# Neighbourhood attention: the product of weights and reciprocal sums on GpSimd instead of VectorE

## The chip, the cores and the metric

The kernel runs on one core of one Trainium2 chip. The metric is the device time of one execution in microseconds (us). Before the change three runs took 2624.79, 2625.38 and 2626.43 us; the median is 2625.38 us.

## The reference, cut to what matters

The program computes two blocks of a network on 512 tokens of 1024 features in float32: four mixers (retention with neighbourhood attention, a state-space mixer, latent attention, an mLSTM) and four feed-forward layers. The change touches the first mixer alone, and in it the neighbourhood attention on the grid of 8 rows by 64 columns:

```
sc = einsum('brqhd,brwchd->bhrqwc', qb, kb) + bias      # a query sees 8 rows x 16 columns
sc = where(valid, sc, -inf)
pr = softmax(sc)                                        # exp(sc - max) / sum
return einsum('bhrqwc,brwchd->brqhd', pr, vb)
```

Beside it the mixer's other half, retention, ends in a normalisation over each head (`mu`, `var`, `rsqrt`), a gain and a gate; then `concatenate([ret_out, na_out]) @ w_out` follows.

## The kernel before, in words

The program is written engine by engine, with the order of each engine's instructions and all semaphores by hand. Most of its time is TensorE's: products of weight blocks with activations, each split in a high and a low part.

The neighbourhood attention is 16 items (`NA_ITEMS`): four pairs of heads by four blocks of 16 query columns. An item has two heads, e = 0 and 1, and for each 128 queries by 256 keys. The engines go over the items in step n:

- TensorE (`pe_softmax`, step n): waits for the maxima of item n-1 (`item_max`), multiplies queries and keys of item n into bank 0 and bank 1 (L1295, the scores); multiplies the turned weights of item n-3 with the values (L1326); waits for each head's normalised weights of item n-2 (`item_normed`) and transposes them (L1315); then runs the hook.
- VectorE (`dve_softmax`, step n): for each head adds the bias table to the scores and takes the maximum in one instruction (L1376); negates the two maxima (L1380, `item_max`); then, for item n-1, takes the reciprocal of the two sums (L1387) and multiplies the weights by it, one instruction of 128x256 for each head (L1389, `item_normed`); then runs the hook.
- ScalarE (`act_softmax`, step n): copies the transposed weights of item n-2 from their bank (L1351), takes the exponential of item n with its sum (L1360, two heads), then runs the hook.

Three buffers hold the weights (`na_soft`), two hold each item's columns of maxima and sums (`stat`).

The hooks carry the normalisation of the retention half, in six steps for each of four feature tiles j (`gn_steps`): in step 3j+2 TensorE multiplies by a centring matrix (L1646) and ScalarE copies the result (L1665); GpSimd squares it (L1720); in step 3j+5 TensorE takes the variance (L1649); in step 3j+6 ScalarE takes the reciprocal root in two instructions (L394, L395); in step 3j+7 VectorE multiplies by it and by gain and gate (L1657, L1658). Four copies of finished outputs by ScalarE (L1706), and in two steps the split of an output tile for the next product (ScalarE L592, then VectorE L597), are in the hooks too. From step 15 on TensorE fills gaps with the next product (`ab_out`, L374 to L376).

GpSimd (`pool_na_tables`) builds the bias tables for all eight heads (L1727, 24 instructions), which ends before the items need them, and then has only the four squares left in this stage. Items 0 and 1 are started inside the last two steps of the retention loop, where L1612 is VectorE's work.

Of the kernel before, what the change touches and what calls it, by code (L numbers as in the profile page):

```python
# [165 lines left out]
def build(nc, A, stop=None):  # L166

    with ExitStack() as ctx:
        sems = {}

        def sem(name):
            if name not in sems:
                sems[name] = ctx.enter_context(nc.semaphore(name))
            return sems[name]
# [707 lines left out]
            return 32 * f + m + 1  # L882

        POOL_SUMS, COPIES, DVE_SUMS = 1 + 4 * PAIRS + MLP_TILES, 5 + 2 * PAIRS, 7 + 2 * PAIRS
        TOKEN_SUMS = ("t3", "t1", "t2", "t4")
        SUM_AT = {"s1": 0, "s2": 1, "s3": 2, "s4": 3}

# [10 lines left out]
            return COPIES * f + 5 + 2 * n + 2  # L898

        def w_summed(f, n):  # L900
            return DVE_SUMS * f + 7 + 2 * n + 1

        def c_summed(f, n):
            return DVE_SUMS * f + 7 + 2 * n + 2

        def token_low(f, t):
            return DVE_SUMS * f + 3 + TOKEN_SUMS.index(t) + 1

        TOKEN_AT = {"t4": 0, "t3": 1, "t1": 2, "t2": 3}
        HALF_N = SEQ // 2  # L910
# [48 lines left out]
        def pool_pairs(pool, f):  # L959
            pool.wait_ge(sem("sum_copied"), COPIES * f + 1)  # L960
            pool.wait_ge(sem("norm_added"), 6 + 2 * f)
            b = over_a[:, :].rearrange("p (k s) -> p k s", k=4)
            pool.tensor_tensor(mT[:, token("t1")].rearrange("p (k s) -> p k s", k=4), b[:, :, HALF_N:SEQ], b[:, :, 0:HALF_N],
                               ALU.subtract).then_inc(sem("sum_pool"), 1)
            pool.wait_ge(sem("sum_pool"), POOL_SUMS * f + 1)
            pool.wait_ge(sem("sum_dve"), DVE_SUMS * f + 1)
            for n in range(PAIRS):
                wait_block(pool, f, n, 0)
                wait_block(pool, f, n, 1)
                if n:  # L970
                    pool.wait_ge(sem("w_lo"), split(f, "s1", n - 1))
                pool.tensor_tensor(sum_raw("s1"), block_raw(f, n, "a21"), block_raw(f, n, "a22"), ALU.add)\
                    .then_inc(sem("sum_pool"), 1)
                if n:
                    pool.wait_ge(sem("w_lo"), split(f, "s2", n - 1))
                pool.wait_ge(sem("sum_pool"), pool_summed(f, "s1", n))
                pool.tensor_tensor(sum_raw("s2"), sum_raw("s1"), block_raw(f, n, "a11"), ALU.subtract)\
                    .then_inc(sem("sum_pool"), 1)
                if n:
                    pool.wait_ge(sem("w_lo"), split(f, "s3", n - 1))  # L980
                pool.tensor_tensor(sum_raw("s3"), block_raw(f, n, "a11"), block_raw(f, n, "a21"), ALU.subtract)\
                    .then_inc(sem("sum_pool"), 1)
                if n:
                    pool.wait_ge(sem("w_lo"), split(f, "s4", n - 1))
                pool.wait_ge(sem("sum_pool"), pool_summed(f, "s2", n))
                pool.tensor_tensor(sum_raw("s4"), block_raw(f, n, "a12"), sum_raw("s2"), ALU.subtract)\
                    .then_inc(sem("sum_pool"), 1)

            pool.wait_ge(sem("norm_rstd"), 6 + 2 * f)
            for m in range(MLP_TILES):  # L990
                pool.wait_ge(sem("mlp_hidden"), relu_done(f, m))
                pool.tensor_tensor(tile(m), tile(m), rstd[:, :], ALU.mult).then_inc(sem("sum_pool"), 1)  # L992

        def act_mlp_up(act, f):
# [7 lines left out]
            def token_high(t):  # L1002
                if t == "t1":
                    act.wait_ge(sem("sum_pool"), POOL_SUMS * f + 1)
                else:
                    act.wait_ge(sem("sum_dve"), DVE_SUMS * f + {"t3": 1, "t2": 2, "t4": 3}[t])
                act.activation(tok_hi[:, token(t)], mT[:, token(t)], ACT.Copy).then_inc(sem("sum_copied"), 1)

            def high(q, n):
# [107 lines left out]
        def dve_mlp_up(dve, f):  # L1117
# [3 lines left out]
            def tokens(t):  # L1121

                half = slice(0, HALF_N) if t == "t4" else slice(HALF_N, SEQ)
                if t == "t3":
                    dve.wait_ge(sem("sum_copied"), COPIES * f + 1)
                if t == "t2":
                    dve.wait_ge(sem("sum_pool"), POOL_SUMS * f + 1)
                if t == "t4":
                    dve.wait_ge(sem("sum_dve"), DVE_SUMS * f + 2)
                    dve.wait_ge(sem("norm_sum"), norm + 1)  # L1130
                for j in range(4):
                    less = over_a[:, j * SEQ + HALF_N:(j + 1) * SEQ] if t == "t3" else mT[:, token("t1" if t == "t2" else "t2", j)]
                    ins = dve.scalar_tensor_tensor(out=mT[:, token(t, j)], in0=xt(4 + j)[:, half], scalar=col(g, g0 + 4 + j),
                                                   in1=less, op0=ALU.mult, op1=ALU.subtract)
                ins.then_inc(sem("sum_dve"), 1)

            def token_lows(t):
                dve.wait_ge(sem("sum_copied"), COPIES * f + 1 + TOKEN_SUMS.index(t) + 1)
                if t == "t1":
                    dve.wait_ge(sem("sum_dve"), DVE_SUMS * f + 2)  # L1140
                if t == "t2":
                    dve.wait_ge(sem("sum_dve"), DVE_SUMS * f + 3)
                dve.tensor_tensor(tok_lo[:, token(t)], mT[:, token(t)], tok_hi[:, token(t)], ALU.subtract)\
                    .then_inc(sem("sum_dve"), 1)

# [215 lines left out]
                                       scale=items[n]["scale"][e], accum_out=stat(1, n, e)).then_inc(sem("item_exp"), 1)  # L1361
                hook(act, n)

        def dve_softmax(dve, n0, items, soft, ready, hook, part=None):
            N = len(items)
            lo, hi = part or (0, N + 1)
            for n in range(lo, hi):
                if n < N:
                    it = items[n]
                    w = it["w"]  # L1370
                    ready(dve, n)
                    if n >= 3:
                        dve.wait_ge(sem("item_transposed"), n0 + n - 2)
                    for e in range(2):
                        dve.wait_ge(sem("item_scored"), 2 * (n0 + n) + e + 1)
                        dve_order(dve, dve.tensor_tensor_reduce(out=soft(n, e)[:, 0:w], in0=bank[e][:, 0:w], in1=it["bias"][e],  # L1376
                                                                scale=1.0, scalar=NEG, op0=ALU.add, op1=ALU.max,
                                                                accum_out=stat(2, n, e)))
                    if it["minus"] is None:
                        dve.tensor_scalar(stat(0, n, 0, 2), stat(2, n, 0, 2), -1.0, None, ALU.mult).then_inc(sem("item_max"), 1)  # L1380
                    else:
                        dve.tensor_tensor(stat(0, n, 0, 2), stat(2, n, 0, 2), it["minus"], ALU.mult).then_inc(sem("item_max"), 1)
                if n >= 1:
                    m = n - 1
                    w = items[m]["w"]
                    dve.wait_ge(sem("item_exp"), 2 * (n0 + m) + 2)
                    dve_order(dve, dve.reciprocal(stat(3, m, 0, 2), stat(1, m, 0, 2)))  # L1387
                    for e in range(2):
                        dve.tensor_scalar(soft(m, e)[:, 0:w], soft(m, e)[:, 0:w], stat(3, m, e), None, ALU.mult)\  # L1389
                            .then_inc(sem("item_normed"), 1)  # L1390
                hook(dve, n)

        def stat(kind, n, e, count=1):
            c = 4 + kind * 4 + n % 2 * 2 + e
            return stats[:, c:c + count]
# [314 lines left out]
        def pool_na_tables(pool):  # L1710
# [4 lines left out]
            def squares(j):  # L1715
                pool.wait_ge(sem("gn_centered"), j + 1)
                if j:
                    pool.wait_ge(sem("gn_var"), j)
                y = tile(RV + j)
                pool.tensor_tensor(sq[:, 0:SEQ], y, y, ALU.mult).then_inc(sem("gn_sq"), 1)  # L1720

            for h in range(8):
                if h in (4, 6):
                    pool.wait_ge(sem("ret_scored"), 8 * (h // 2))
                for v, shift in enumerate((16, 8, 0)):
# [2 lines left out]
                                       wide(arena[:, a:a + 1], [15, SPAN], [1, ROWS]),  # L1728
                                       wide(ab["namask"][:, v * 256:v * 256 + 1], [8, SPAN], [1, ROWS]), ALU.add)\
                        .then_inc(sem("na_table"), 1)  # L1730
            for j in range(4):
                squares(j)

        def pe_ab_up(pe):
            def between(pe, m):
# [24 lines left out]
        def dve_na(dve, part):  # L1760
            def ready(dve, n):
                dve.wait_ge(sem("na_table"), 6 * (n // 4) + 6)
                if n == 1:
                    dve.wait_ge(sem("ret_valued"), 15)

            def hook(dve, n):
                gn_dve(dve, n)
                if n in (11, 14):
                    dve_low_part(dve, "ab_out", At(n // 3 - 3))
            dve_softmax(dve, 0, NA_ITEMS, na_soft, ready, hook, part)  # L1770

        def pe_ab(pe):
            pe_retention(pe)
# [1672 lines left out]
```

## Time and profile before

| | before |
|---|---|
| median of three runs | 2625.38 us |
| the profiled execution's own time | 2624.66 us |
| its span | 2622.7 us |
| TensorE busy | 2583.3 us (98%) |
| VectorE busy | 1682.1 us (64%) |
| ScalarE busy | 1287.1 us (49%) |
| GpSimd busy | 503.7 us (19%) |
| first scores of the attention | 203.06 us from the span's start |
| scores of its last item | 241.51 us |

The span is the profiled part of an execution. Busy shares are means over all stages. TensorE's granted clock is at its full level through the span (mean 0.998). In the timelines below an instruction's start is the time from the span's start, and its end is the start plus the duration; where two instructions are merged (x2), the duration is that of both. TensorE's ends are modelled, and its rows may overlap by some tenths of a microsecond.

### The profile page before, as it was taken

To read this page: it belongs to the slowest core of one execution; us is meant where nothing else is said; L and a number is where in the kernel's file an instruction comes from. 1 tells how busy PE (TensorE), PEld (TensorE's weight loads), DVE (VectorE), ACT (ScalarE), POOL (GpSimd) and SP (SyncE) were. 2 spreads that over 40 slices of the span, in tenths; PEclk is the share of its full clock that TensorE was granted. 3 is DMA by queue.
4 is the path that set the end of the run, shared out by engine and by line. 5 is a ranking of instruction groups with operands and counts; after the bars stand their busy time and mean duration, and the time that the engine had idled before them with its cause. 6 is when DMAs were issued, how large, how long until landed. Compare 5 with 4: busy or idle time off the path is not lost. (4 is left out here: it accounts for less than half of the span.)

```text
span 2622.7 us, 35151 instructions
## 1 busy us (share of the span) xinstructions
PE 2583.3 (98%) x12530; PEld 2047.4 (78%) x12530; DVE 1682.1 (64%) x2288; ACT 1287.1 (49%) x2138; POOL 503.7 (19%) x366
## 2 busy tenths in 40 slices
PE   9999999999999999999999999999999999999999
PEld 7855788888786557788888776789988777889887
DVE  4476677643988785677653787578733536678633
ACT  3326544333547894444333587457533425557432
POOL 0021100000114781100000130035810002045800
PEclk9999999999999999999999999999999999999999
DMA  5320222222244442222222220133232321233222
GB/s 212 105 79 17 95 97 97 98 97 98 82 131 129 121 129 80 81 96 96 96 97 98 92 73 1 65 102 108 83 111 97 103 86 49 97 105 113 81 96 96
DMA packets 72991, 248.39 MB, mean 95 GB/s; under 512 B 8076, under 2 KB 8204, under 8 KB 72496
## 3 DMA queue, kind: packets, MB, share of 16 engines
q1 hardware_dynamic: 71792, 238.53, 27.4%
q0 software_dynamic: 944, 8.40, 0.8%
q8 instruction: 67, 1.10, 0.2%
q14 instruction: 44, 0.36, 0.0%
q10 hardware_dynamic: 144, 0.00, 0.0%
HBM read 242.56 MB, written 2.24 MB: 93 GB/s over the span
## 5 line engine op out<-in xcount | busy, mean ns | idle before, releaser
L356 DVE TENSOR_TENSOR wlo<-wraw,whi 128x1024 fp32r<-128x1024 f32 x357 | 458.2, 1285 | 429.7 <-ACT whi L333 428.8
L374 PE MATMUL bank<-hnhi,whi 128*128 128x512 f32 (+1 forms) x1664 | 654.1, 393 | 2.0 <-DVE arena L1954 1.2
L375 PE MATMUL bank<-hnlo,whi 128*128 128x512 f32 (+1 forms) x1664 | 638.4, 384 | 0.0
L333 ACT ACTIVATE whi<-wraw 128x1024 fp32r<-128x1024 f32 x361 | 379.9, 1055 | 480.6 <-DMA wraw<-in_w 480.5
L376 PE MATMUL bank<-hnhi,wlo 128*128 128x512 f32 x1568 | 611.0, 390 | 0.0
L374 PE MATMUL bank<-ahi,whi 128*128 128x512 f32 x1184 | 463.1, 391 | 1.0 <-DVE alo L597 0.5
L375 PE MATMUL bank<-alo,whi 128*128 128x512 f32 x1184 | 460.9, 389 | 0.0
L376 PE MATMUL bank<-ahi,wlo 128*128 128x512 f32 x1184 | 460.8, 389 | 0.0
L374 PEld LDWEIGHTS bank<-hnhi,whi 128*128 128x128 f32 x1664 | 312.8, 188 | 93.7 <-issue 32.8
L375 PEld LDWEIGHTS bank<-hnlo,whi 128*128 128x128 f32 x1664 | 313.0, 188 | 64.0 <-issue 4.8
L376 PEld LDWEIGHTS bank<-hnhi,wlo 128*128 128x128 f32 x1568 | 294.3, 188 | 62.5
L374 PEld LDWEIGHTS bank<-ahi,whi 128*128 128x128 f32 x1184 | 222.3, 188 | 51.2 <-DVE alo L597 3.8
L376 PEld LDWEIGHTS bank<-ahi,wlo 128*128 128x128 f32 x1184 | 222.2, 188 | 46.5
L375 PEld LDWEIGHTS bank<-alo,whi 128*128 128x128 f32 x1184 | 222.3, 188 | 45.9 <-issue 0.5
L777 POOL TENSOR_TENSOR xT<-xT,mT 128x512 f32<-128x512 f32 x20 | 33.9, 1726 | 873.2 <-DVE mT L769 873.2
L818 ACT ACTIVATE mT<-mT,cols 128x512 f32<-128x512 f32 x88 | 71.8, 816 | 223.3 <-DVE mT L516 223.3
L592 ACT ACTIVATE ahi<-arena 128x512 fp32r (+1 forms) x140 | 87.9, 630 | 136.1 <-PE bank L376 135.0
L597 DVE TENSOR_TENSOR alo<-arena,ahi 128x512 fp32r<-128x512 f32 x140 | 110.4, 788 | 66.7 <-ACT ahi L592 66.5
L841 DVE SCALAR_TENSOR_TENSOR mT<-mT,cols 128x511 f32<-128x511 f32 x88 | 66.1, 751 | 97.3 <-ACT mT L818 97.3
L992 POOL TENSOR_TENSOR arena<-arena,rstd 128x512 f32<-128x512 f32 x64 | 110.7, 1768 | 0.0
L516 DVE TENSOR_TENSOR arena<-bank,rstd 128x512 f32<-128x512 f32 (+3 forms) x48 | 36.5, 763 | 110.3 <-PE bank L376 98.5
L1149 DVE TENSOR_TENSOR quarter_lo<-over_a,whi 128x512 fp32r<-128x512 f32 x96 | 83.5, 873 | 23.6 <-ACT whi L1021 22.9
(350 smaller groups left out, 3894.0 us busy)
## 6 DMA issues: line engine op xcount, KB each, us to landing
wraw<-in_w SPq DMA_DIRECT2D x410, 512.0 KB, 3.3
arena<-cs_scratch SPq DMA_DIRECT2D x20, 512.0 KB, 5.9
over_a<-cs_scratch SPq DMA_DIRECT2D x12, 512.0 KB, 6.1
arena<-in_rpb POOLq DMA_DIRECT2D x1, 2880.0 KB, 14.6
out_dram<-xT SPq DMA_DIRECT2D x8, 256.0 KB, 2.0
arena<-in_t_step POOLq DMA_DIRECT2D x2, 897.0 KB, 5.4
mT<-arena SPq DMA_DIRECT2D x28, 64.0 KB, 2.0
arena<-in_t_ab POOLq DMA_DIRECT2D x1, 1472.0 KB, 7.2
```

Of the source, the lines that this page charges most:

```text
L333: act.activation(whi[:, slot * BLOCK:(slot + 1) * BLOCK], wraw[:, slot * BLOCK:(slot + 1) * BLOCK], ACT.Copy).then_inc(sem("w_hi"), 1)
L356: dve.tensor_tensor(wlo[:, slot * BLOCK:(slot + 1) * BLOCK], wraw[:, slot * BLOCK:(slot + 1) * BLOCK], whi[:, slot * BLOCK:(slot + 1) * BL ...
L374: pe.matmul(out, wh, ah, start=start, stop=False)
L375: pe.matmul(out, wh, al, start=False, stop=False)
L376: return pe.matmul(out, wl, ah, start=False, stop=stop)
L516: dve.tensor_tensor(out, src, by, ALU.mult).then_inc(sem(done), 1)
L592: act.activation(ahi[:, c:c + SEQ], src(k), ACT.Copy).then_inc(sem("a_hi"), 1)
L597: dve.tensor_tensor(alo[:, c:c + SEQ], MIXERS[name][0](k), ahi[:, c:c + SEQ], ALU.subtract).then_inc(sem("a_lo"), 1)
L818: act.activation(cbuf(m), ubuf(m), ACT.Identity, bias=col("fb", m + 44 * f), scale=col("fw", m + (132 * f + 44))).then_inc(sem("ffn_center ...
L841: dve.scalar_tensor_tensor(out=c[:, 1:SEQ], in0=u[:, 0:SEQ - 1], scalar=col("fw", m + 132 * f), in1=c[:, 1:SEQ], op0=ALU.mult, op1=ALU.add ...
L992: pool.tensor_tensor(tile(m), tile(m), rstd[:, :], ALU.mult).then_inc(sem("sum_pool"), 1)
L1149: dve.tensor_tensor(quarter_low(q, n), src, quarter_hi(f, q, n), ALU.subtract).then_inc(sem("w_lo"), 1)
```

## The change: who multiplies, and in which order

VectorE still takes the reciprocal of the two sums (L1387), but signals it to GpSimd through the semaphore `sum_dve` and no longer waits for its own result. The two multiplications of each item go to GpSimd, which waits for that signal and then signals `item_normed` twice. GpSimd's four squares, which stood after the tables, are put behind the multiplications of items 1, 4, 7 and 10. The semaphore `sum_dve` is used later in the program too; its counts there are raised by 16 (`DVE_BASE`), in seven places of which one is shown.

```diff
         def token_low(f, t):
-            return DVE_SUMS * f + 3 + TOKEN_SUMS.index(t) + 1
+            return DVE_BASE + DVE_SUMS * f + 3 + TOKEN_SUMS.index(t) + 1
...
-        def dve_softmax(dve, n0, items, soft, ready, hook, part=None):
+        def dve_softmax(dve, n0, items, soft, ready, hook, part=None, by_pool=False):
...
                     dve.wait_ge(sem("item_exp"), 2 * (n0 + m) + 2)
-                    dve_order(dve, dve.reciprocal(stat(3, m, 0, 2), stat(1, m, 0, 2)))
-                    for e in range(2):
+                    if by_pool:
+                        dve.reciprocal(stat(3, m, 0, 2), stat(1, m, 0, 2)).then_inc(sem("sum_dve"), 1)
+                    else:
+                        dve_order(dve, dve.reciprocal(stat(3, m, 0, 2), stat(1, m, 0, 2)))
+                    for e in range(0 if by_pool else 2):
                         dve.tensor_scalar(soft(m, e)[:, 0:w], soft(m, e)[:, 0:w], stat(3, m, e), None, ALU.mult)\
                             .then_inc(sem("item_normed"), 1)
...
-            for j in range(4):
-                squares(j)
+            for m in range(len(NA_ITEMS)):
+                pool.wait_ge(sem("sum_dve"), m + 1)
+                for e in range(2):
+                    pool.tensor_scalar(na_soft(m, e), na_soft(m, e), stat(3, m, e), None, ALU.mult).then_inc(sem("item_normed"), 1)
+                if m % 3 == 1 and m < 12:
+                    squares(m // 3)
...
-            dve_softmax(dve, 0, NA_ITEMS, na_soft, ready, hook, part)
+            dve_softmax(dve, 0, NA_ITEMS, na_soft, ready, hook, part, by_pool=True)
```

The second user of `dve_softmax`, the latent attention later in the program, keeps the multiplications on VectorE.

## Rows read from the trace of the kernel before

**Rows 1.** Who waited for whom, 203 to 252 us: total us, times, longest us.

```profile
PEld bank L1295 <- DVE stats L1380: 7.2, 12, 1.1
DVE mT L1376 <- PE bank L1295: 5.3, 12, 1.7
```

**Rows 2.** Busy time by stretch: length, PE, PEld, DVE, ACT, POOL, clock, DMA.

```profile
221.96:226.06 4.10, 3.60 (x21) 1.79 (x21) 3.69 (x13) 3.57 (x11) 0.00 (x0) 1.00 0.00 0
228.09:230.12 2.03, 1.88 (x17) 1.14 (x17) 1.72 (x9) 2.02 (x6) 0.00 (x0) 1.00 0.00 0
241.51:250.00 8.49, 8.41 (x59) 5.87 (x58) 5.08 (x17) 5.78 (x14) 0.00 (x0) 1.00 0.01 2
```

**Rows 3.** Timeline of TensorE: start us, us, engine, line; steps 10, 14 and 15.

```profile
228.09 0.70 PE L1295 MATMUL bank<-arena 64*128 64x256 f32 x4 [0.15 <-DVE stats L1380]
229.31 0.66 PE L1315 MATMUL bank<-base_t,mT 128*128 128x128 f32 x4
230.12 0.70 PE L1295 MATMUL bank<-arena 64*128 64x256 f32 x4 [0.15 <-DVE stats L1380]
...
241.51 0.70 PE L1295 MATMUL bank<-arena 64*128 64x256 f32 x4
...
242.73 0.66 PE L1315 MATMUL bank<-base_t,mT 128*128 128x128 f32 x4
```

**Rows 4.** Timeline of VectorE: the plain step 10.

```profile
227.94 0.16 DVE L1387 RECIPROCAL stats<-stats 128x2 f32<-128x2 f32 x1
228.13 0.61 DVE L1389 TENSOR_SCALAR mT<-mT,stats 128x256 f32<-128x256 f32 x2
228.96 0.42 DVE L1376 CUSTOM_DVE_ANT_0 mT<-bank,arena 128x256 f32<-128x256 f32 x1 [0.21 <-PE bank L1295]
...
229.89 0.17 DVE L1380 TENSOR_SCALAR stats<-stats 128x2 f32<-128x2 f32 x1
```

**Rows 5.** Timeline of all engines, steps 7 to 9.

```profile
221.81 0.16 DVE L1387 RECIPROCAL stats<-stats 128x2 f32<-128x2 f32 x1
...
221.99 0.64 ACT L395 ACTIVATE rstd<-rstd 128x512 f32<-128x512 f32 x1
222.00 0.61 DVE L1389 TENSOR_SCALAR mT<-mT,stats 128x256 f32<-128x256 f32 x2
...
222.66 0.69 DVE L1657 TENSOR_TENSOR arena<-arena,rstd 128x512 f32<-128x512 f32 x1
...
224.98 0.17 DVE L1380 TENSOR_SCALAR stats<-stats 128x2 f32<-128x2 f32 x1
...
226.06 0.70 PE L1295 MATMUL bank<-arena 64*128 64x256 f32 x4
...
226.19 0.57 ACT L1665 ACTIVATE arena<-bank 128x512 f32<-128x512 f32 x1
...
226.84 1.04 POOL L1720 TENSOR_TENSOR sq<-arena 128x512 f32<-128x512 f32 x1 [7.37 <-ACT arena L1665]
...
227.86 0.17 DVE L1380 TENSOR_SCALAR stats<-stats 128x2 f32<-128x2 f32 x1
```

**Rows 6.** Timeline of VectorE: steps 14 and 15.

```profile
241.29 0.17 DVE L1380 TENSOR_SCALAR stats<-stats 128x2 f32<-128x2 f32 x1
...
242.09 0.68 DVE L597 TENSOR_TENSOR alo<-arena,ahi 128x512 fp32r<-128x512 f32 x1
```

**Rows 7.** Timeline, VectorE beside GpSimd: step 3, and a later stage.

```profile
211.23 1.04 POOL L1720 TENSOR_TENSOR sq<-arena 128x512 f32<-128x512 f32 x1 [11.16 <-ACT arena L1665]
...
211.48 0.81 DVE L1380 TENSOR_SCALAR stats<-stats 128x2 f32<-128x2 f32 x1
...
299.56 0.75 DVE L435 SCALAR_TENSOR_TENSOR hnlo<-xT,cols,hnhi 128x512 fp32r<-128x512 f32 x1
299.79 8.47 POOL L777 TENSOR_TENSOR xT<-xT,mT 128x512 f32<-128x512 f32 x5 [63.77 <-DVE mT L769]
...
300.88 1.13 DVE L435 SCALAR_TENSOR_TENSOR hnlo<-xT,cols,hnhi 128x512 fp32r<-128x512 f32 x1
```

**Rows 8.** GpSimd's instructions by shape: count, busy us, mean ns, idle before.

```profile
L1727 POOL TENSOR_TENSOR arena<-arena 128x256 f32<-128x256 f32 x12 | 8.1, 706 | 18.0 <-PE bank L1547 18.0
...
L2915 POOL TENSOR_TENSOR arena<-arena 128x256 f32<-128x256 f32 x3 | 3.3, 1106 | 7.1 <-DVE arena L3109 7.1
L2912 POOL COPY arena<-arena 128x512 f32<-128x512 f32 x3 | 1.8, 612 | 68.2 <-DVE arena L3109 68.2
```

More of the change, by code:

```diff
@@ L884, in build @@
         POOL_SUMS, COPIES, DVE_SUMS = 1 + 4 * PAIRS + MLP_TILES, 5 + 2 * PAIRS, 7 + 2 * PAIRS
+        DVE_BASE = 16
         TOKEN_SUMS = ("t3", "t1", "t2", "t4")
@@ L900, in w_summed @@
         def w_summed(f, n):
-            return DVE_SUMS * f + 7 + 2 * n + 1
+            return DVE_BASE + DVE_SUMS * f + 7 + 2 * n + 1
         def c_summed(f, n):
-            return DVE_SUMS * f + 7 + 2 * n + 2
+            return DVE_BASE + DVE_SUMS * f + 7 + 2 * n + 2
         def token_low(f, t):
-            return DVE_SUMS * f + 3 + TOKEN_SUMS.index(t) + 1
+            return DVE_BASE + DVE_SUMS * f + 3 + TOKEN_SUMS.index(t) + 1
         TOKEN_AT = {"t4": 0, "t3": 1, "t1": 2, "t2": 3}
@@ L965, in pool_pairs @@
             pool.wait_ge(sem("sum_pool"), POOL_SUMS * f + 1)
-            pool.wait_ge(sem("sum_dve"), DVE_SUMS * f + 1)
+            pool.wait_ge(sem("sum_dve"), DVE_BASE + DVE_SUMS * f + 1)
             for n in range(PAIRS):
@@ L1005, in token_high @@
                 else:
-                    act.wait_ge(sem("sum_dve"), DVE_SUMS * f + {"t3": 1, "t2": 2, "t4": 3}[t])
+                    act.wait_ge(sem("sum_dve"), DVE_BASE + DVE_SUMS * f + {"t3": 1, "t2": 2, "t4": 3}[t])
                 act.activation(tok_hi[:, token(t)], mT[:, token(t)], ACT.Copy).then_inc(sem("sum_copied"), 1)
@@ L1128, in tokens @@
                 if t == "t4":
-                    dve.wait_ge(sem("sum_dve"), DVE_SUMS * f + 2)
+                    dve.wait_ge(sem("sum_dve"), DVE_BASE + DVE_SUMS * f + 2)
                     dve.wait_ge(sem("norm_sum"), norm + 1)
@@ L1139, in token_lows @@
                 if t == "t1":
-                    dve.wait_ge(sem("sum_dve"), DVE_SUMS * f + 2)
+                    dve.wait_ge(sem("sum_dve"), DVE_BASE + DVE_SUMS * f + 2)
                 if t == "t2":
-                    dve.wait_ge(sem("sum_dve"), DVE_SUMS * f + 3)
+                    dve.wait_ge(sem("sum_dve"), DVE_BASE + DVE_SUMS * f + 3)
                 dve.tensor_tensor(tok_lo[:, token(t)], mT[:, token(t)], tok_hi[:, token(t)], ALU.subtract)\
```

## The prediction

> **What bounds the kernel now.** The page comes first: TensorE is busy for 2583.3 of 2622.7 us, so the whole program has under 40 us of it idle, and what the change can touch lies between 203.06 and about 250 us. I then read that stretch in four views. The waits [rows 1] show what the steps turn on: TensorE's scores wait for VectorE's negated maxima (7.2 us in 12 places), and VectorE's maxima wait for TensorE's scores (5.3 us in 12 places). Nothing there waits for L1389. The table of stretches [rows 2] gives the two sorts of step: a plain one of 2.03 us, and one with the centring and variance products of 4.10 us; ScalarE has 2.02 us of work in the plain one, so it too is nearly full. The timelines give the loop. In step 10 TensorE starts the scores at 228.09, VectorE starts the maximum at 228.96 after standing idle for 0.21 us, starts the negation at 229.89, and TensorE starts the next scores at 230.12 [rows 3, 4]. VectorE's multiplications run from 228.13 to 228.74, in the time that VectorE would spend waiting for those scores. The reader is to see that the plain period is scores, two maxima, negation, and that the removed work is in none of them.
>
> **What the change removes.** Sixteen pairs of L1389, 0.61 us each [rows 4], 9.8 us of VectorE in all, and a wait on the reciprocal. Its worth on the path, by the kind of step:
> - Plain steps: 0. VectorE waits for the scores with or without it, 0.21 us now and about 0.85 us then.
> - Steps 7, 10 and 13, whose hook has L1657: 0. L1389 ends at 222.00 + 0.61 = 222.61, but L1657 needs ScalarE's L395 too, which ends at 221.99 + 0.64 = 222.63; L1657 starts at 222.66 [rows 5]. The cover of the removed work goes and the other wait stands there at the same moment.
> - Step 14, whose hook has L597: the maximum of item 15 could start some 0.3 us earlier, but no scores come after item 15, and ScalarE is still at other work then: 0. If that cover were not there it would be 0.3 us.
>
> **What it adds.** A pair of GpSimd instructions for each item, behind the reciprocal. The trace has no GpSimd instruction with a tensor and a column as inputs. The nearest rows [rows 8]: a copy of 128x512 takes 0.612 us, so half of it, 0.31, bounds one of 128x256 from below; the two-input form of 128x256 takes 0.71 (table building), and 1.11 in a stage where VectorE works beside it, which bounds it from above. I take 0.50, between the halved copy (which halves its fixed part too) and 0.71. The hand-over to GpSimd is 0.08: L1665 ends at 226.76 and L1720 starts at 226.84 [rows 5].
>
> A plain step then: reciprocal done at 227.94 + 0.16 = 228.10, the first head done at 228.10 + 0.08 + 0.50 = 228.68, the second at 229.18. The transposes start at 229.31 [rows 3], the second head's about 0.3 later, at 229.6. So 0.13 us and more to spare: cost 0. At 0.31 each it is 228.80, at 0.71 it is 229.60 (still about 0), at 1.11 it is 230.40, 0.8 late (below, the slow rival). Step 2 has its transposes earlier, and may lose 0.2 us, but the negation of item 3 is held until 212.29 by the first squares in any case [rows 7]: 0. The moved squares wait for L1665 behind the items before them as before, and the next item's reciprocal comes after they end: 0 by themselves.
>
> **The two engines at once.** Step 3 of the trace shows what else comes with it. L1380, a two-column instruction of 0.17 us, took 0.81: it started at 211.48 and ended at 212.29, when GpSimd's L1720 (211.23 + 1.04 = 212.27) had ended. L435, with two tensors in, takes 0.75 alone and 1.13 beside L777 [rows 7]. So some of VectorE's instructions stand still while GpSimd works. (The Trainium skill, "SBUF — State Buffer", section "Who interferes with whom", says that a VectorE instruction with two SBUF inputs, or in a two-port mode, and a GpSimd instruction that reads SBUF exclude each other, whichever begins first. By that rule L1657, L1658, L597 and L1380 are exposed and L1376, which reads a bank, is not; these two row pairs agree. Without the rule's two-input half the next sum would be 0.)
>
> In steps 7, 10 and 13 the pair on GpSimd runs just where L1657 wants to start. Item 6: reciprocal done 221.97, GpSimd's first 222.05 to 222.55, second to 223.05; L1657 wanted 222.66 and starts about 0.39 late. What that costs [rows 5]: the negation of item 8 moves from 224.98 to 225.37; the scores of item 9 come at 226.06 for TensorE's own reasons, so nothing is lost there. But ScalarE's exponential and L1665 follow, L1720 moves from 226.84 to 227.23 and ends at 228.27, and L1380 of item 9, due at 227.86, stands until then: some 0.36 on the path, since the next scores wait for it. The same once more three steps later (0.36). The third time there are no squares, but L1380 of item 14, at 241.29 + 0.17, is only 0.05 us ahead of the scores at 241.51 [rows 3, 6], so 0.39 - 0.05 = 0.34. Then L597: VectorE now starts it right behind the reciprocal at 241.53, GpSimd is held until 242.22, its second head is done at 243.22, and the transposes at 242.73 want it at about 243.0: 0.2. After that TensorE is busy for 8.41 of 8.49 us [rows 2], so a late start there is not made good.
>
> **Sum.** -0 + 0 + 0.36 + 0.36 + 0.34 + 0.2 = +1.3 us. On the profiled execution, 2624.66 + 1.3 = 2625.9; its time lies 0.7 below the median of the runs, so in medians 2625.38 + 1.3 = 2626.7 us. That is +0.05%, well inside the 0.2% (5.3 us) that I take as what a measurement of this kernel tells from no change.
>
> **Rivals.**
> 1. The engines miss each other (time as before, 2625.4). With 0.31 us for one multiplication the pair ends at 222.05 + 0.62 = 222.67, just when L1657 is ready, and every collision above falls away. (The Trainium skill, "GPSIMD Engine Reference", section 4.1, calls one-input work on GpSimd roughly line-rate, which speaks for this rival.) Against it: the halved copy leaves out the fixed part.
> 2. It is faster after all (2623.2). If VectorE's lateness, not ScalarE's L395, set L1657's start, three hooks would give 0.62 us each and the step with L597 0.3: 3 x 0.62 + 0.3 = 2.2 us. For it: L1389 and L395 end within 0.02 us of each other, so the trace alone doesn't say which is the deeper cause. Against it: ScalarE is full in these steps and would have to be earlier as well.
> 3. Slower (2633): GpSimd's multiplication is the new link. It decides from about 0.7 us for one: then reciprocal to second head, 0.08 + 1.4, exceeds the 1.5 us from 228.10 to 229.6. At 1.11 the second head's transposes start at 230.40 and the next scores some 0.25 later, at 230.65 instead of 230.12, so 0.5 us a step over about nine plain steps, 4.6 us; and L1657 finds the lock taken for 0.5 to 1.6 us three times, another 1.5 to 4.8. Together 6 to 9 us, 2631 to 2634. For it: 1.106 us was measured for this size [rows 8]. Against it: that form has two inputs, and the same form took 0.71 elsewhere.
>
> **How the numbers follow.** Forecast (slower by about 1 us, from 0.4 to 2.5) 0.55; rival 1 0.20; rival 2 0.10; rival 3 0.15. The forecast and the first two rivals lie within 0.2% of before; of rival 3 two thirds lie beyond it, and a gain over 5.3 us would need more idle time than ScalarE leaves. So faster 0.02, same 0.87, slower 0.11. The range for eight in ten leaves out the top of rival 3 and the bottom of rival 2, with 0.6 us for the scatter of the runs: 2623.8 to 2631.0.
>
> **What would show it.** In the profile after: plain steps still 2.03 us with VectorE idle for some 0.8 us before L1376; GpSimd's multiplications near 0.5 us each, ending before the transposes start; L1657 (or its idle time) longer or later by 0.4 us behind GpSimd in steps 7, 10 and 13; L1380 of items 9 and 12 over 0.17 us; the last scores near 242.6 instead of 241.51. Plain steps over 2.2 us, or TensorE's L1315 waiting for GpSimd, would prove rival 3; last scores before 241.0, rival 2. The forecast is wrong if the time is outside 2625.8 to 2628.

## The result, and the profile after

Twenty runs of each kernel: before 2625.36 us (2624.36 to 2627.4), after 2628.93 us (2625.83 to 2631.71), ratio 1.0014 with a 95% interval of 1.0008 to 1.002. The change makes the kernel slower by 3.6 us, inside the 0.2% and inside the range of the prediction, but 2.7 times the +1.3 us that was forecast. Beside the experiments further down, one run of the kernel before took 4299.17 us at a mean granted clock of 0.556; it is left out of every ratio.

The profiled execution after took 2630.92 us, with a span of 2629.0 us, 6.3 us more than before. Only half of that is the change's: in the trace the attention takes, from the start of its first scores to the start of its last values, 46.95 us before (203.07 to 250.02) and 50.10 us after (204.75 to 254.85). This length is what I compare from here on. It is the same within 0.03 us in a second profile of the changed kernel (50.07), where whole runs of one kernel differ by up to 6 us. The rest of the 6.3 us, 1.68 us ahead of the attention and 1.47 behind it, stands where no code changed; the last section says what it is.

Who waited for whom in the stage after, 203 to 256 us (columns as in [rows 1]):

```profile
POOL mT L1738 <- DVE stats L1389: 14.5, 15, 7.6
DVE mT L1377 <- PE bank L1296: 14.2, 13, 2.6
...
PEld bank L1296 <- DVE stats L1381: 5.1, 7, 1.1
PEld bank L1316 <- POOL mT L1738: 4.1, 8, 0.7
```

Against [rows 1], TensorE's scores wait less for the negation (7 times for 12), and a wait is new: the transposes, L1316, wait for GpSimd's multiplication, L1738. Lines have moved: the scores are L1296, the negation L1381, the reciprocal L1389, the hook's L1657 and L1658 are L1661 and L1662.

The stretches that answer to [rows 2], step 8, step 10 and what follows the last scores:

```profile
225.52:229.52 4.00, 3.82 (x22) 1.78 (x21) 2.55 (x8) 3.40 (x12) 2.73 (x3) 1.00 0.00 0
231.55:233.91 2.36, 2.02 (x16) 1.12 (x16) 1.12 (x7) 2.33 (x7) 2.05 (x3) 1.00 0.00 0
245.54:254.03 8.49, 7.94 (x56) 5.46 (x56) 3.59 (x10) 5.78 (x14) 5.83 (x6) 1.00 0.01 2
```

The plain step went from 2.03 to 2.36 us, the long one from 4.10 to 4.00. Step 10 in the timeline, which answers to [rows 3, 4]:

```profile
231.41 0.15 DVE L1389 RECIPROCAL stats<-stats 128x2 f32<-128x2 f32 x1
...
231.55 0.70 PE L1296 MATMUL bank<-arena 64*128 64x256 f32 x4 [0.16 <-DVE stats L1381]
231.66 1.83 POOL L1738 TENSOR_SCALAR mT<-mT,stats 128x256 f32<-128x256 f32 x2 [0.19 <-DVE stats L1389]
...
232.77 0.44 PE L1316 MATMUL bank<-base_t,mT 128*128 128x128 f32 x2
...
233.54 0.44 PE L1316 MATMUL bank<-base_t,mT 128*128 128x128 f32 x2 [0.33 <-POOL mT L1738]
233.91 0.70 PE L1296 MATMUL bank<-arena 64*128 64x256 f32 x4
```

The reader is to see the second L1316: before, the four transposes of an item ran in one go and the negation was the last thing that the next scores waited for. Now GpSimd's pair ends at 231.66 + 1.83 = 233.49, the second head's transposes start at 233.54, and the next scores follow them directly. One multiplication takes 0.92 us, not 0.50.

The largest single loss is in step 2, where the transposes of item 0 come soonest after its reciprocal. Before:

```profile
207.59 0.70 PE L1295 MATMUL bank<-arena 64*128 64x256 f32 x4 [0.21 <-DVE stats L1380]
208.23 0.66 PE L1315 MATMUL bank<-base_t,mT 128*128 128x128 f32 x4
```

and after:

```profile
209.28 0.70 PE L1296 MATMUL bank<-arena 64*128 64x256 f32 x4 [0.21 <-DVE stats L1381]
209.40 1.84 POOL L1738 TENSOR_SCALAR mT<-mT,stats 128x256 f32<-128x256 f32 x2 [7.63 <-DVE stats L1389]
...
210.47 0.41 PE L1316 MATMUL bank<-base_t,mT 128*128 128x128 f32 x2 [0.48 <-POOL mT L1738]
...
211.29 0.44 PE L1316 MATMUL bank<-base_t,mT 128*128 128x128 f32 x2 [0.41 <-POOL mT L1738]
```

There both heads wait for GpSimd.

Step 7, which answers to [rows 5]:

```profile
225.23 0.63 ACT L395 ACTIVATE rstd<-rstd 128x512 f32<-128x512 f32 x1
...
225.29 2.08 POOL L1738 TENSOR_SCALAR mT<-mT,stats 128x256 f32<-128x256 f32 x2 [0.20 <-DVE stats L1389]
...
225.89 0.69 DVE L1661 TENSOR_TENSOR arena<-arena,rstd 128x512 f32<-128x512 f32 x1 [0.69 <-ACT rstd L395]
...
226.62 0.85 DVE L1662 SCALAR_TENSOR_TENSOR arena<-arena,cols 128x512 f32<-128x512 f32 x1
```

L1661 was to be held by 0.39 us until GpSimd was done. It starts 0.03 us after L395 ends, in the middle of GpSimd's work, and takes its usual 0.69. GpSimd's pair is 0.25 us longer instead (2.08 for 1.83), and L1662 0.10 (0.85 for 0.75). The next L1661 takes 0.69 too; the third takes 0.79 and the fourth, at 251.09, 0.94, both started within 0.04 us of L395's end.

In step 12 a square stands behind two multiplications, and the negation of item 12 waits for it (before: 0.17 us):

```profile
239.18 1.04 POOL L1724 TENSOR_TENSOR sq<-arena 128x512 f32<-128x512 f32 x1
...
239.71 0.54 DVE L1381 TENSOR_SCALAR stats<-stats 128x2 f32<-128x2 f32 x1
```

Behind the last scores (step 15) GpSimd starts beside L597:

```profile
245.35 0.67 DVE L597 TENSOR_TENSOR alo<-arena,ahi 128x512 fp32r<-128x512 f32 x1
245.53 4.16 POOL L1738 TENSOR_SCALAR mT<-mT,stats 128x256 f32<-128x256 f32 x4 [1.27 <-DVE stats L1389]
...
247.77 0.44 PE L1316 MATMUL bank<-base_t,mT 128*128 128x128 f32 x2 [0.40 <-POOL mT L1738]
```

From GpSimd's start to the second head's transposes there are 2.24 us, where step 10 has 1.88.

All fifteen steps between scores, before and after, as differences of the starts of L1295 and L1296: the ones that changed are step 2 (2.08 to 3.24), 3 (2.67 to 2.51), 4, 7, 10 and 13 (2.03 to 2.36), 5 (3.53 to 3.74), 8 (4.10 to 4.00), 11 (4.09 to 3.99), 12 (2.03 to 2.40) and 14 (3.24 to 2.88); from the last scores to the last values 8.51 became 9.31. Added up: 1.16 + 4 x 0.33 + 0.21 + 0.80 = 3.49 where transposes are late or have just been (in step 5 part of the 0.21 is the values, which wait for ScalarE's copy of step 4's late transposes), 0.37 in step 12, and 0.16 + 0.10 + 0.10 + 0.36 = 0.72 given back in steps 3, 8, 11 and 14, where a step that starts later finds other waits already over (that reading is argued from the rows, not tested). 3.49 + 0.37 - 0.72 = 3.14 us.

### The profile page after: what moved, and what is told of

Same layout as the page of the kernel before. It is cut to its first block and busy times, and to the rows that moved or that the text cites. A ratio compares the mean times of both kernels' runs of the same rounds, so it can differ in the third digit from the quotient of the medians.

```text
span 2629.0 us, 35151 instructions
## 1 busy us (share of the span) xinstructions
PE 2588.1 (98%) x12530; PEld 2048.7 (78%) x12530; DVE 1673.8 (64%) x2256; ACT 1288.0 (49%) x2138; POOL 533.6 (20%) x398
## 3 DMA queue, kind: packets, MB, share of 16 engines
HBM read 242.56 MB, written 2.24 MB: 93 GB/s over the span
## 5 line engine op out<-in xcount | busy, mean ns | idle before, releaser
L777 POOL TENSOR_TENSOR xT<-xT,mT 128x512 f32<-128x512 f32 x20 | 33.9, 1728 | 862.2 <-DVE mT L769 862.2
L597 DVE TENSOR_TENSOR alo<-arena,ahi 128x512 fp32r<-128x512 f32 x140 | 110.6, 790 | 65.7 <-ACT ahi L592 65.4
```

Source lines behind the costliest of these rows:

```text
L597: dve.tensor_tensor(alo[:, c:c + SEQ], MIXERS[name][0](k), ahi[:, c:c + SEQ], ALU.subtract).then_inc(sem("a_lo"), 1)
```

## The experiments

Two theories: the new link (GpSimd's two multiplications are too long for the 1.5 us between the reciprocal and the second head's transposes) and the collisions (VectorE and GpSimd stand in each other's way, the forecast's). "Length" is first scores to last values, from one profile each; medians are over 11 runs of each kernel unless said otherwise, beside 27 to 33 of the kernel before on the same chip.

| kernel | length, us | against before | median less before's |
|---|---|---|---|
| before | 46.95 | | |
| after, again | 50.07 | +3.12 | +2.5 |
| half width | 47.59 | +0.64 | +0.6 |
| one head | 47.22 | +0.27 | -0.2 |
| idle work | 49.14 | +2.19 | +1.6 |
| unlinked | 47.67 | +0.72 | +0.6 |
| ten items | 48.95 | +2.00 | +2.8 |
| scaled identity | 52.86 | +5.91 | +5.9 |
| double | 78.44 | +31.49 | +32 |
| nobody multiplies | 46.97 | +0.02 | -0.2 |
| before, held squares | 47.35 | +0.40 | +1.2 |
| after, held squares | 57.21 | +10.26 | +7.6 |
| one head, held squares | 47.59 | +0.64 | +0.8 |

The length follows the median within 1 us, but for one kernel (after, held squares: 10.26 against 7.6). Only the changed kernel was profiled twice, and its length repeats to 0.03 us; a step that no edit reaches repeats as well (step 6 takes 2.03 us in 13 of the 14 profiles, the scaled identity's apart). Differences of a few tenths are read from the length and the steps alone; by whole runs none of them stands out of the scatter.

**After, again**, without an edit:

> The changed kernel once more, beside the kernel before on the same chip. Theory (new link): one GpSimd multiplication of 128x256 takes 0.91 us, two of them are ready 1.9 us after the reciprocal where 1.5 us are to spare; the attention takes 3.1 us more from its first scores to its last values, in the profile 1.2 us of it at item 0, 0.33 us in each of steps 4, 7, 10 and 13, 0.37 us in step 12 and 0.8 us behind the last scores. Rival (collisions of VectorE and GpSimd, the forecast's): the lost time stands at L1661/L1662 and L1381. Both expect +3 to +4 us in the median (2628.4 to 2629.4 where before is 2625.4); the profile tells them apart.

Measured: 2627.4 against 2624.95 us, ratio 1.0009 (1.0000 to 1.0018), less than the +3 to +4 us that both theories expected in the median, and the steps of the first profile to 0.02 us. The loss stands at L1316, not at L1661.

**Half width**

```diff
-pool.tensor_scalar(na_soft(m, e), na_soft(m, e), stat(3, m, e), None, ALU.mult)
+pool.tensor_scalar(na_soft(m, e)[:, 0:P], na_soft(m, e)[:, 0:P], stat(3, m, e), None, ALU.mult)
```

> GpSimd multiplies only the first 128 of each 256 columns; the other half of the weights stays unnormalised (left out). New link: an instruction of some 0.5 us, the pair ready 1.1 us after the reciprocal, inside the 1.5 us: steps 4, 7, 10, 13 back to 2.03 us, the whole attention within 0.6 us of before, median +0 to +0.8 us. Collisions: GpSimd still works when L1661, L1662, L597 and L1381 want to start, so +1 us or more stays, near the 1.3 us of the forecast, and steps 12 and 14 to 15 are longer than before.

Measured: 2625.57 us, ratio 1.0003 (0.9994 to 1.0012). One instruction takes 0.60 us. All plain steps are back at 2.03 us; +0.51 stands in step 2, -0.16 in step 3 and +0.26 behind the last scores, as the new link has it. The collision stands on GpSimd's side:

```profile
222.56 1.69 POOL L1738 TENSOR_SCALAR mT<-mT,stats 128x128 f32<-128x128 f32 x2 [0.84 <-DVE stats L1389]
```

The pair takes 1.19 us elsewhere; here L1661, which starts at 223.15, gets ahead of its second half and GpSimd waits 0.5 us, which nobody needs. The collisions' +1 us is not there. This run makes GpSimd's work shorter as well as the link, so it fits a collision smaller than forecast too; the run without the link, below, parts the two.

**One head**: head 0 stays on VectorE.

```diff
...
+dve.tensor_scalar(soft(m, 0)[:, 0:w], soft(m, 0)[:, 0:w], stat(3, m, 0), None, ALU.mult).then_inc(sem("item_normed"), 2)
...
-for e in range(2):
-    pool.tensor_scalar(na_soft(m, e), na_soft(m, e), stat(3, m, e), None, ALU.mult).then_inc(sem("item_normed"), 1)
+pool.tensor_scalar(na_soft(m, 1), na_soft(m, 1), stat(3, m, 1), None, ALU.mult).then_inc(sem("pool_normed"), 1)
```

> Head 0 is multiplied by VectorE (as before), head 1 by GpSimd, with a semaphore of its own. The result is complete. New link: head 1 is ready 0.08 + 0.91 = 1.0 us after the reciprocal, in time; the attention within 0.5 us of before, median +0 to +0.8 us. Collisions: VectorE's multiplication and GpSimd's want the same moment, one of the two is held by up to 0.9 us, and L1661 too; +1 to +3 us.

Measured: 2624.78 us, ratio 0.9998 (0.9989 to 1.0007). The plain steps are 2.03 us.

```profile
L1744 POOL TENSOR_SCALAR mT<-mT,stats 128x256 f32<-128x256 f32 x16 | 17.1, 1072 | 22.7 <-DVE stats L1392 22.7
```

Here GpSimd's instruction takes 1.07 us instead of 0.92, beside VectorE's own multiplication, and is still in time but for step 2, which stays 0.39 us longer than before.

**Idle work**: VectorE multiplies as before, GpSimd does the same amount for nobody.

```diff
-for e in range(0 if by_pool else 2):
+for e in range(2):
...
-pool.tensor_scalar(na_soft(m, e), na_soft(m, e), stat(3, m, e), None, ALU.mult).then_inc(sem("item_normed"), 1)
+pool.tensor_scalar(sq[:, SEQ + e * 256:SEQ + e * 256 + 256], base_t[:, 0:256], stats[:, 0:1], None, ALU.mult).then_inc(sem("dummy"), 1)
```

> VectorE multiplies both heads as before; GpSimd does two multiplications of the same size at the same moment on other data that nobody reads (identity and ones, times a constant). So GpSimd's work is there and its result is not a link. New link: the time of before, +0 to +0.5 us (GpSimd still delays the squares by its queue). Collisions: all of the loss stays, +3 to +4 us, with L1391 (VectorE's multiplications) or L1661 and L1662 longer than before.

Measured: 2626.55 us, ratio 1.0007 (0.9998 to 1.0016). The new link's +0 to +0.5 fell, but this is not the changed kernel's loss either. L1316 waits for GpSimd nowhere; VectorE is what is late:

```profile
L1381 DVE TENSOR_SCALAR stats<-stats x16: 168/268/978, 204.7 to 245.8; 128x2 f32<-128x2 f32 x16
```

(Least, median and longest duration in ns.) The negation takes longer than its 0.17 us in nine of sixteen items, and VectorE's pair of multiplications takes 0.84 us instead of 0.61. The large losses are behind GpSimd's squares (negations of 0.76 and 0.98 us, one pair of multiplications of 1.56). GpSimd's work meets VectorE's multiplications here, which the changed kernel doesn't have, so this run doesn't price the changed kernel's collisions. The next one does:

**Unlinked**: nobody multiplies the weights, GpSimd works on other data, the transposes wait for the reciprocal.

```diff
-pe.wait_ge(sem("item_normed"), 2 * (n0 + n) + e + 1)
+pe.wait_ge(sem("sum_dve"), n + 1)
...
-pool.tensor_scalar(na_soft(m, e), na_soft(m, e), stat(3, m, e), None, ALU.mult).then_inc(sem("item_normed"), 1)
+pool.tensor_scalar(sq[:, SEQ + e * 256:SEQ + e * 256 + 256], base_t[:, 0:256], stats[:, 0:1], None, ALU.mult).then_inc(sem("item_normed"), 1)
```

> As the changed kernel, but GpSimd's two multiplications go from other data to other memory, and TensorE's transposes wait for VectorE's reciprocal instead of them. The normalisation of the weights is left out. VectorE does no multiplication either, so GpSimd's work lies beside the same instructions of VectorE as in the changed kernel (before: first scores to last values 46.95 us, changed: 50.1). New link: 47.0 to 47.4 us. Collisions, as the forecast sized them: at least 48.0 us, with L1661 and L1662 late by 0.4 us three times.

Measured: 2625.63 us, ratio 1.0002 (0.9993 to 1.0011), length 47.67, between the two expectations. Cutting the link takes back 50.10 - 47.67 = 2.4 of the 3.1 us. The 0.72 us that stay are collisions, but not those of the forecast: L1664 (L1661's place) starts within 0.04 us of L395's end each time. They are at the negation, behind GpSimd's squares: steps 3, 9 and 12 are 0.27, 0.23 and 0.60 us longer than before, and steps 11 and 14 give 0.36 back. Steps 9 and 12:

```profile
227.39 1.04 POOL L1727 TENSOR_TENSOR sq<-arena 128x512 f32<-128x512 f32 x1
...
228.05 0.40 DVE L1384 TENSOR_SCALAR stats<-stats 128x2 f32<-128x2 f32 x1
...
235.91 1.04 POOL L1727 TENSOR_TENSOR sq<-arena 128x512 f32<-128x512 f32 x1
...
236.21 0.77 DVE L1384 TENSOR_SCALAR stats<-stats 128x2 f32<-128x2 f32 x1
```

The squares stand behind a pair of 1.83 us in GpSimd's queue and so slip onto the next negation, which is held until they end (236.21 + 0.77 = 236.98, against 235.91 + 1.04 = 236.95). This is what it costs to put `squares` behind the multiplications in one queue; a changed kernel with the squares elsewhere in the queue was not run.

**Ten items**: GpSimd takes only the items that had cost the changed kernel's steps nothing, or next to nothing. (The expectation says that their transposes didn't wait. Those of items 6 and 9 did, a little: L1316 took 0.88 us for 0.66, in steps 8 and 11, which became shorter all the same.)

```diff
+BY_POOL = (1, 3, 4, 6, 7, 9, 10, 12, 14, 15)
...
-for e in range(2):
-    pool.tensor_scalar(na_soft(m, e), na_soft(m, e), stat(3, m, e), None, ALU.mult).then_inc(sem("item_normed"), 1)
+if m in BY_POOL:
+    for e in range(2):
+        pool.tensor_scalar(na_soft(m, e), na_soft(m, e), stat(3, m, e), None, ALU.mult).then_inc(sem("pool_normed"), 1)
```

> GpSimd multiplies only for items 1, 3, 4, 6, 7, 9, 10, 12, 14 and 15, whose transposes didn't wait for it in the changed kernel's profile; VectorE multiplies for items 0, 2, 5, 8, 11 and 13. The result is complete. New link: the loss is a matter of which items have 1.9 us between reciprocal and transposes, so ten of sixteen cost nothing, first scores to last values 47.0 to 47.5 us, median within 0.8 us of before. Collisions: the squares and L1381 still meet in step 12, and GpSimd still works beside L1661's steps; 48 us or more.

Measured: 2627.81 us, ratio 1.0007 (0.9998 to 1.0016), length 48.95. My expectation, 47.0 to 47.5, fell. Step 5 is 0.62 us longer than before, steps 8 and 11 0.22 and 0.23, step 12 0.36, and 0.76 stands behind the last scores. Item 3, whose transposes had waited 0.1 us at most, now waits 0.40:

```profile
214.45 3.78 POOL L1748 TENSOR_SCALAR mT<-mT,stats 128x256 f32<-128x256 f32 x4 [1.67 <-DVE stats L1396]
```

```profile
215.52 0.41 PE L1323 MATMUL bank<-base_t,mT 128*128 128x128 f32 x2
216.33 0.44 PE L1323 MATMUL bank<-base_t,mT 128*128 128x128 f32 x2 [0.40 <-POOL mT L1748]
```

Its first pair ends 1.8 to 1.9 us after 214.45, and the transposes want it at 215.8. In the changed kernel the item before had already made TensorE late, and that hid this one. Item 1 waits as well now (0.36 us). Which item waits is thus not a property of the item; the stall moves to the next one when it is taken away.

**Scaled identity**: GpSimd multiplies the identity, TensorE turns and scales in one product.

```diff
-pool.tensor_scalar(na_soft(m, e), na_soft(m, e), stat(3, m, e), None, ALU.mult)
+pool.tensor_scalar(na_diag(m, e), ident, stat(3, m, e), None, ALU.mult)
...
-mm = pe.transpose(out[:, at + c:at + c + P], soft(n, e)[:, c:c + P], ident)
+mm = pe.matmul(out[:, at + c:at + c + P], soft(n, e)[:, c:c + P], na_diag(n, e), start=True, stop=True)
```

> GpSimd multiplies the 128x128 identity by the reciprocals (0.60 us for one, as at 128 columns in the run with half the width) and TensorE multiplies the weights by that in place of the plain transpose. The result is complete. New link: as with half the width, 47.6 us from first scores to last values, +0.6 of it in step 2 and behind the last scores, median +0 to +1 us. If TensorE's product with this matrix costs more than the transpose, L1316's rows show it and the steps grow by it. Collisions: the same as with half the width, so this run doesn't tell them apart; it is the cheapest complete form of the work on GpSimd.

Measured: 2630.93 us, ratio 1.0022 (1.0013 to 1.0031).

```profile
220.64 1.16 PE L1323 MATMUL bank<-sq,mT 128*128 128x128 f32 x8
```

The product takes eight rows and 1.16 us for an item where the transpose takes four and 0.66: 0.5 us x 16 on the busiest engine, of which 5.91 us reach the length. GpSimd's 0.60 us was in time but for item 0, where the product waits 0.16 us.

**Double**: each multiplication done twice, first to other memory.

```diff
+pool.tensor_scalar(sq[:, SEQ + e * 256:SEQ + e * 256 + 256], na_soft(m, e), stat(3, m, e), None, ALU.mult).then_inc(sem("dummy"), 1)
+pool.wait_ge(sem("dummy"), 2 * m + e + 1)
 pool.tensor_scalar(na_soft(m, e), na_soft(m, e), stat(3, m, e), None, ALU.mult).then_inc(sem("item_normed"), 1)
```

> GpSimd does each multiplication twice, first to other memory, then in place. New link: a pair takes about 3.8 us, more than a plain step, so GpSimd is the bound from item to item: 16 x 3.8 + 4 x 1.04 = 65 us of it in the stage, first scores to last values 62 to 67 us, median +15 to +20 us. Collisions: the loss grows only with the places where the engines meet, twice as much work, at most twice the loss, +6 to +8 us.

Measured over 4 runs: 2657.0 us, ratio 1.0117 (1.0102 to 1.0133), length 78.44. Collisions as I had priced them can't do this. The new link's 62 to 67 was low by 11 us too. It counted GpSimd's own work alone: its first multiplication starts 4.65 us after the first scores, its last one ends 2.5 us before the last values, and around the squares it stands idle for 4.3 us, waiting for TensorE's variance and VectorE's next reciprocal. TensorE, left idle, was also granted less clock: after 1.50 and 1.42 us of waiting the stretch from 208 to 218 us has 0.66 of it, and scores take 1.23 us instead of 0.70.

```profile
208.00:218.00 10.00, 7.09 (x30) 3.55 (x28) 2.27 (x12) 4.02 (x13) 9.32 (x11) 0.66 0.01 2
```

**Nobody multiplies**

```diff
-for m in range(len(NA_ITEMS)):
-    pool.wait_ge(sem("sum_dve"), m + 1)
-    for e in range(2):
-        pool.tensor_scalar(na_soft(m, e), na_soft(m, e), stat(3, m, e), None, ALU.mult).then_inc(sem("item_normed"), 1)
...
-pe.wait_ge(sem("item_normed"), 2 * (n0 + n) + e + 1)
+pe.wait_ge(sem("sum_dve"), n + 1)
```

> Nobody multiplies: VectorE takes the reciprocal and the transposes wait for that; GpSimd has only its four squares. The normalisation of the weights is left out. This prices the removed work alone, which the forecast put at 0. If it is hidden: 46.6 to 47.0 us from first scores to last values (before 46.95), median within 0.5 us of before. If VectorE's multiplications were on the path (rival 2 of the forecast): 44.8 us or less, the steps with L1661 shorter by 0.6 us. It is also the floor for any way of taking the multiplications off VectorE.

Measured: 2624.71 us, ratio 0.9999 (0.9990 to 1.0008), length 46.97, no step off by more than 0.01 us. The multiplications on VectorE cost nothing where they were, so in this schedule there is nothing to gain by taking them off VectorE.

**Before, held squares**

```diff
 pool.wait_ge(sem("gn_centered"), j + 1)
+pool.wait_ge(sem("item_max"), 3 * j + 4)
```

> The kernel before with one more wait: GpSimd starts each square only when the negation of the item after (item_max at 3j + 4) is done, so L1720 can't hold L1380. If the lock at L1380 is what costs 0.64 us in step 3, that step falls from 2.67 to 2.1 us, first scores to last values 46.3 to 46.5 us, and the squares still come in time for the variance product. If not, 46.9 us or more.

Measured: 2626.11 us, ratio 1.0003 (0.9994 to 1.0012), length 47.35, where I expected 46.3 to 46.5. Step 3 fell from 2.67 to 2.03 us, so the lock at the negation is real and cost 0.64; but each square now meets VectorE's multiplications instead, and steps 4, 7, 10 and 13 grow to 2.6 (steps 8, 11 and 14 give 1.24 of that back):

```profile
211.60 1.50 DVE L1389 TENSOR_SCALAR mT<-mT,stats 128x256 f32<-128x256 f32 x2
```

A pair that takes 0.61 us [rows 4] takes 1.50 beside L1721's 211.64 to 212.68.

**After, held squares** (the same edit):

> The changed kernel with the same wait before each square. The wait also holds the multiplications queued behind the square on GpSimd. New link alone: the loss from the waits of the transposes stays (2.4 us), the 0.5 us at L1381 of items 3 and 12 goes, but item 3j+2 may be multiplied up to 1 us later, so 49.0 to 50.5 us from first scores to last values (changed kernel 50.1).

Measured over 9 runs: 2632.43 us, ratio 1.0027 (1.0017 to 1.0037), length 57.21 and far above my 49.0 to 50.5. A pair of multiplications queues behind each held square; the transposes of step 4 wait 0.89 and 0.40 us for it. Step 5 takes 6.45 us for 3.53, and in it the clock is at its lower level (0.72 from 212 to 224 us).

**One head, held squares** (the same edit):

> Head 0 on VectorE, head 1 on GpSimd, with the held squares. The result is complete. One head each cost 0.27 us over before; the lock of 0.47 us at item 3 goes, unless the multiplication of item 2 behind the held square comes too late for its transposes (0.5 us to spare): 46.5 to 47.2 us from first scores to last values, median within 0.5 us of before.

Measured: 2625.64 us, ratio 1.0004 (0.9995 to 1.0013), length 47.59, above my 46.5 to 47.2. Step 3 fell to 2.03 us as it should, but the multiplication behind each held square comes too late for its transposes, which wait 0.29 us for it in steps 4, 7, 10 and 13, and the steps are 0.45 longer. None of the twelve is faster than the kernel before by more than 0.2 us in the median or at all in the length.

## Why the prediction was right or wrong

The direction (slower, by less than 0.2%), the range and "no gain in the removed work" held. The size did not: +1.3 forecast, +3.6 measured. By the forecast's own sign (wrong outside 2625.8 to 2628) the likeliest case is wrong, and so is its mechanism: it put the loss at collisions, and 2.4 of 3.1 us are TensorE's transposes waiting for GpSimd.

- Removed work, 0: right. The run in which nobody multiplies has the length of before to 0.02 us, and rival 2 falls.
- One multiplication at 0.50 us: wrong, and the step that failed, for with it the plain steps were priced at 0. It takes 0.915 us (1.83 for two), 0.60 at 128 columns, by these two points about 0.29 us and 2.5 ns a column, and the plain steps 4, 7, 10 and 13 lose 0.33 us each. I had halved a copy (0.61 for 512 columns) and leaned towards it; a tensor times a column costs more on GpSimd than the two-input form of that shape did while alone (0.71), and still lies inside the bounds of 0.31 and 1.11. The copy of 512 columns takes 0.61 us in all, so at most 1.2 ns a column.
- The threshold of about 0.7 us, from which GpSimd is the link: not contradicted, and bracketed only. At 2 x 0.60 and with one head (1.07 us) the plain steps keep 2.03 us, at 2 x 0.915 they don't.
- Rival 3's price: 0.5 us over nine plain steps at 1.11. At 0.915 it is 0.33 in four of them, because the items whose reciprocal comes in a long step have time to spare (item 4: GpSimd starts at 219.53, the transposes at 222.35). Its mechanism is what happened, below its price of 6 to 9 us; I had given it 0.15.
- Collisions at L1661, 3 x 0.35: wrong. L1661 never waits to start. It takes 0.69, 0.69, 0.79 and 0.94 us in the profile after, and GpSimd's pair gets longer beside the first two (2.08 and 2.07 us for 1.83). (By the two-input half of the rule that the Trainium skill gives in "SBUF — State Buffer", section "Who interferes with whom", L1661 would have waited for GpSimd's instruction; against this one-input multiplication the trace disagrees: it starts 0.6 us into the pair and takes 0.69.) The rows behind the forecast were of another kind: L1380 stood behind a two-input square, and L435 [rows 7] was slowed beside the two-input L777, not stopped. Nor is 299.56 L435 alone, since L777 starts at 299.79.
- The arithmetic of the two 0.36: by the forecast's own rows 0.26. The square would end at 228.27 and the negation with it at 228.29, where it ended at 227.86 + 0.17 = 228.03. The sum would have been +1.1.
- The moved squares, 0 by themselves: wrong by 0.37 us, at L1381 of item 12, which the forecast had named but priced through L1661. Item 9, which it had named too, keeps 0.17 us in the profile after. In the run without the link the squares cost 0.72 us net.
- Step 2, 0 because the squares hold the negation in any case: wrong, +1.16 and then -0.16. The squares follow TensorE's centring product, so they slipped along with it.
- After the last scores, 0.2: 0.80. Part of it is the same 0.915 us, and part the forecast's own collision: beside L597 the pair takes 0.36 us longer than in step 10 (2.24 for 1.88 until the second head's transposes). How the 0.80 divides was not tested.

In the signs shown beforehand, "L1315 waiting for GpSimd, plain steps over 2.2 us" named rival 3, and that is what the profile has. The time lies in the range by luck: +3.6 falls in the gap between the likeliest case (0.4 to 2.5) and rival 3 (6 to 9), and the range, drawn up to the foot of rival 3 at 2631.0, covers that gap.

## What to carry to other kernels

Before moving work off an engine, find the wait that it shortens; here the idle time of 0.21 us before L1376 already said that there was none. An operation whose result is wanted at a fixed time needs its duration on the new engine from a row of the same operation; where none exists, the forecast is as wide as the bounds. And a stall that shows at every third item isn't confined to those: whole loops are to be checked against the spare time of each.

## What the runs showed of the hardware

- VectorE's negation and multiplication stand until GpSimd's two-input square ends, and the square keeps its 1.04 us (the negation's 0.17 us becomes 0.40 to 1.07, the pair of multiplications' 0.61 becomes 1.50; both end with or behind the square).
- GpSimd's one-input multiplication beside VectorE's two-input L1661 doesn't hold back VectorE's start; VectorE's instruction takes up to 0.25 us longer, GpSimd's pair 0.25 us (0.5 us at 128 columns). Beside VectorE's one-input multiplication both are slowed and neither stands: 0.84 us for VectorE's pair (0.61 alone), 1.07 for GpSimd's single one (0.92 alone). The negation beside it took 0.39 instead of 0.17.
- A product with a scaled identity in float32 takes twice the instructions of a transpose of the same shape (1.16 against 0.66 us).
- TensorE's granted clock falls to its lower level (1.2 GHz for 2.4) for some microseconds in every profile near 174 us, also in the one before, so that the clock isn't at its full level through the whole span there. In both of the profiles shown, TensorE had waited 2.59 us for VectorE just before. How long it stays there differs from run to run, before the change is reached:

```profile
172.00:182.00 10.00, 8.51 (x32) 3.03 (x32) 6.12 (x11) 1.60 (x3) 2.00 (x2) 0.83 0.00 0
```

```profile
172.00:182.00 10.00, 8.21 (x24) 2.64 (x24) 5.57 (x9) 1.91 (x4) 2.30 (x3) 0.66 0.00 0
1656.00:1664.00 8.00, 6.50 (x42) 5.32 (x43) 3.89 (x12) 3.33 (x9) 0.00 (x0) 0.79 0.01 2
```

The first is the profile before, the second the one after (the clock stands behind the five engines: 0.83 and 0.66). The first scores come at 203.07 and 204.75, and in the profiles of the experiments anywhere from 202.44 to 203.25. Near 1658 us the profile after has another fall that the one before has not (1.00 there), but of the experiments' profiles some show one there and some do not, the second profile of the changed kernel among the latter. Whole runs scatter with this clock: runs of the kernel before with a mean granted clock of 0.999 took 2622.62 to 2623.75 us, with 0.998 2623.94 to 2625.3, with 0.997 2625.25 to 2627.6. So the two kernels can be compared at an equal clock: the runs of the kernel before that stood beside the experiments, and the changed kernel's twenty and eleven runs:

| mean granted clock | before, median us (runs) | changed, median us (runs) | difference |
|---|---|---|---|
| 0.999 | 2623.10 (20) | 2626.07 (6) | 2.97 |
| 0.998 | 2624.74 (34) | 2627.81 (9) | 3.08 |
| 0.997 | 2626.45 (35) | 2629.74 (15) | 3.29 |

That is close to the stage's 3.14 us, from whole runs. Of the changed kernel's twenty runs fourteen had 0.997, of its eleven beside the experiments one. Whether the change makes such falls likelier in later stages stays open: the median of twenty lies 0.4 us above what the stage explains (3.57 against 3.14), that of the eleven 0.7 below (2.45).
